# Strassen's seven products for the two branch projections of a hybrid diffusion trunk layer

## The reference

```python
def trunk_layer(x, mod, s_af, s_ab, s_bf, s_bb, col_major, p):
    shift, scale, gate = jnp.split(mod, 3, axis=-1)
    h = rmsnorm(x, p['norm_w']) * (1 + scale) + shift
    proj = h @ p['w_in']
    ...
    o_a, sfa, sba = gdn_branch(qkv, z_a, gate_cols, p, s_af, s_ab)
    o_b, sfb, sbb = lru_branch(x_b, z_b, p, s_bf, s_bb, col_major)
    pa = o_a @ p['w_proj_a']          # (1152 x 1024) @ (1024 x 1024)
    pb = o_b @ p['w_proj_b']          # the same shape
    g_a, g_b = jnp.split(jax.nn.sigmoid(h @ p['w_gate'] + p['b_gate']), 2, axis=-1)
    mixed = (g_a * pa + g_b * pb) @ p['w_out']
    return x + gate * mixed, sfa, sba, sfb, sbb
```

## Time and profile before

| | |
|---|---|
| device time, median of 3 runs | 1491.56 us (1488.91 to 1491.62) |
| span of the profiled execution, first to last instruction | 1486.6 us |
| what lies around the span, median less span | 5.0 us |
| PE busy | 1470.7 us (99%) |
| DVE, ACT, POOL busy | 1016.3, 798.8, 350.0 us |
| branch A and B blocks in the trace | 1177.8 to 1377.6 us, 199.8 us |

### The profile page before, as it was taken

One profiled execution on the slowest core, in us unless ns is written; L12 is line 12 of the kernel. 1 busy time (PEld: TensorE's weight loads), 2 busy tenths in 40 slices (PEclk: granted clock), 3 DMA queues, 4 the chain that ended last, 5 costly groups with the idle time before them and its releaser, 6 DMA issues.

```text
span 1486.6 us, 28072 instructions
## 1 busy us (share of the span) xinstructions
PE 1470.7 (99%) x11376; PEld 1414.7 (95%) x11376; DVE 1016.3 (68%) x1815; ACT 798.8 (54%) x1645; POOL 350.0 (24%) x296
## 2 busy tenths in 40 slices
PE   9999999999999999999999999999999999999997
PEld 8899999999999999999899999999999999999886
DVE  5789897988889898888847744744836711544254
ACT  6574857566584857566476564574576500322111
POOL 3122322232232322132211221221221211342110
PEclk9999999999999999999999999999999999999999
DMA  9322121122213112222311221211212531543132
GB/s 322 112 69 90 33 74 54 45 80 63 79 33 110 30 52 81 88 79 89 114 51 46 82 62 49 82 55 56 82 52 90 170 123 43 169 145 105 43 127 99
DMA packets 122435, 127.46 MB, mean 86 GB/s; under 512 B 6745, under 2 KB 105922, under 8 KB 122306
## 3 DMA queue, kind: packets, MB, share of 16 engines
q1 hardware_dynamic: 122018, 125.34, 26.6%
q10 hardware_dynamic: 288, 0.33, 0.1%
HBM read 105.56 MB, written 20.09 MB: 85 GB/s over the span
## 4 chain that ended last, share of the span: by engine, by line
PE 95%; DVE 2%; SPq 1%; DMA 1%; issue 1%; ACT 0%; POOLq 0%; POOL 0%; DVEq 0%
PE mb L136 16%; PE mb L135 16%; PE mb L134 16%; PE db L134 10%; PE db L136 9%; PE db L135 9%; PE db L1374 2%; PE db L1346 2%; PE db L1390 2%; PE db L1363 2%; PE db L1384 2%; PE db L1008 2%; PE db L1315 1%; PE db L1233 1%; PE db L1194 1%; PE db L1298 1%
## 5 line engine op out<-in xcount | busy, mean ns | idle before, releaser
L134 PE MATMUL mb<-h_hi,w_hi 128*128 128x384 f32 x1080 | 363.0, 336 | 0.0
L135 PE MATMUL mb<-h_lo,w_hi 128*128 128x384 f32 x1080 | 362.9, 336 | 0.0
L136 PE MATMUL mb<-h_hi,w_lo 128*128 128x384 f32 x1080 | 362.9, 336 | 0.0
L134 PE MATMUL db<-h_hi,w_hi 128*128 128x384 f32 x816 | 287.9, 353 | 0.2 <-DVE w_lo L1472 0.2
L136 PE MATMUL db<-h_hi,w_lo 128*128 128x384 f32 x816 | 274.6, 336 | 0.0
L135 PE MATMUL db<-h_lo,w_hi 128*128 128x384 f32 x816 | 274.5, 336 | 0.0
L2074 POOL TENSOR_TENSOR w_lo<-w,w_hi 128x1024 fp32r<-128x1024 f32 x47 | 127.3, 2709 | 459.4 <-ACT w_hi L2109 459.4
L134 PEld LDWEIGHTS mb<-h_hi,w_hi 128*128 128x128 f32 x1080 | 203.0, 188 | 0.1
L136 PEld LDWEIGHTS mb<-h_hi,w_lo 128*128 128x128 f32 x1080 | 203.0, 188 | 0.0
L135 PEld LDWEIGHTS mb<-h_lo,w_hi 128*128 128x128 f32 x1080 | 203.0, 188 | 0.0
L134 PEld LDWEIGHTS db<-h_hi,w_hi 128*128 128x128 f32 x816 | 153.7, 188 | 4.1 <-DVE w_lo L1472 0.7
(11 more groups left out here) (339 smaller groups left out, 2909.4 us busy)
## 6 DMA issues: line engine op xcount, KB each, us to landing
w<-in_w_in SPq DMA_DIRECT2D x48, 512.0 KB, 4.0
d_dt<-decay_rows SPq DMA_DIRECT2D x16, 576.0 KB, 6.7
d_qg<-decay_rows SPq DMA_DIRECT2D x16, 512.0 KB, 4.1
w<-in_w_gate SPq DMA_DIRECT2D x16, 512.0 KB, 4.1
branch_a<-d_kq SPq DMA_DIRECT2D x8, 576.0 KB, 3.3
branch_b<-l_z SPq DMA_DIRECT2D x8, 576.0 KB, 2.8
merge_gates_b<-l_gates SPq DMA_DIRECT2D x8, 576.0 KB, 5.5
m_in<-merge_gates_b SPq DMA_DIRECT2D x8, 576.0 KB
```

The costliest lines, as they stand in the source:

```text
L134: pe.matmul(out, hi, rhi, start=(k == 0), stop=False)
L135: pe.matmul(out, hi, rlo, start=False, stop=False)
L136: return pe.matmul(out, lo, rhi, start=False, stop=(last and stop))
```

## The change

Each branch projection is cut into halves of input channels, output channels and tokens (`KH` = 4 tiles, `TH` = 576 tokens). Instead of eight products of quarters, seven products of sums and differences of quarters are made (Strassen's, in the order 5, 1, 7, 2, 4, 3, 6). A *phase* is one product, with four *items*, one for each tile p of output channels in the half; 2 branches by 7 products by 4 = 56 items w. An item is two banks s of 288 tokens by 4 input tiles by 3 passes = 24 matmuls of 288 columns.

What is new for each item:

- SP loads one or two weight quarters (128x512 each, 256 KB); four raw buffers, `wst` and a new `m_w`.
- POOL forms the weight's sum or difference (`w_sums`, L2164 of the new file, 128x512) for products 5, 1, 7, 2 and 6, and the low part (L2156, 128x512) for all; in its program the sum of an item stands ahead of the low part of the item before.
- ACT makes the high part, 128x512.
- DVE forms the sum of activation quarters (`part_sum`, 128x576) for products 1, 7, 4, 3 and 6 into the `xt` region, and the low part (`part_low`, 128x576), two phases ahead.
- Results leave PSUM in 128x288 pieces: ACT copies them into the accumulator `m_acc` for products 5, 1 and 2, DVE adds them (`add_up`) for products 7, 2, 4, 3 and 6. Products 7 and 6 are accumulated in PSUM on top of the product before them.
- When a tile of the accumulator is complete DVE folds it with the gate from SBUF: `fold_a` (128x1152), `fold_b` (two of 128x1152).

The output projection begins at the last item's end; its weights come through the same four raw buffers, and `mixed` tiles are put in other slots of the activation buffers (`home`).

```diff
+        ORDER = (5, 1, 7, 2, 4, 3, 6)
+        COPIES = {5: ((0, 1, 1.0), (0, 0, -1.0)), 1: ((1, 1, 1.0),), 2: ((1, 0, 1.0),)}
+        ADDS = {7: ((0, 0, ADD),), 2: ((1, 1, SUB),), 4: ((1, 0, ADD), (0, 0, ADD)), 3: ((0, 1, ADD),), 6: ((1, 1, ADD),)}
+        BEHIND = (7, 6)
+        feed = list(range(LAST)) + [NW] + list(range(LAST, NW)) + [NW + k for k in range(1, KT)]
...
+        def wait_ring(eng, w):
+            eng.wait_ge(S["mm"], mm_at(w - 4, 1) if w >= 4 else (NB - 1 + w // 2) * NG)
...
+            for n, item in enumerate(feed):
+                if is_sum(item):
+                    pool.wait_ge(S[raw_sem(n)], raw_count(n))
+                    wait_ring(pool, item)
+                    pool.tensor_tensor(ring(W.wsum, item), raw_of(n)[:, 0:KH, :], raw_of(n)[:, KH:KT, :],
+                                       W_PARTS[combos[item][1]][1]).then_inc(S["w_sum"], 1)
+                if n:
+                    feed_low(n - 1)
...
+            for w in range(NW):
+                if w:
+                    copy_out(w - 1)
...
+                if w + 3 < NW:
+                    feed_high(w + 3)
...
+                if w + 2 * KH < NPH * KH:
+                    part_high(w + 2 * KH)
+                if w >= LAST:
+                    mixed_high(w - LAST)
...
+            def seventh(w):
+                pe.wait_ge(S["w_lo"], was["w_lo"] + NB + at_feed[w] + 1)
+                for s in range(2):
...
+                    for j in range(KH):
+                        if p == 0 and s == 0:
+                            pe.wait_ge(S["r_lo"], was["r_lo"] + n * KH + j + 1)
+                        pe.matmul(out, hi, rhi, start=(j == 0 and m not in BEHIND), stop=False, skip_group_check=True)
+                        pe.matmul(out, hi, rlo, start=False, stop=False, skip_group_check=True)
+                        mm = pe.matmul(out, lo, rhi, start=False, stop=(j == KH - 1), skip_group_check=True)
...
+            for w in range(NW + 1):
+                if w:
+                    add_up(w - 1)
...
+                q = w + 2 * KH
+                if q <= NPH * KH:
+                    part_low(q - 1)
+                if q < NPH * KH:
+                    part_sum(q)
+                if 5 * KH < w <= 7 * KH:
+                    fold_a(w - 5 * KH - 1)
+                elif LAST - KH < w <= LAST:
+                    fold_b(w - LAST + KH - 1)
+                elif w > LAST:
+                    mixed_low(w - LAST - 1)
+            for k in range(KH, KT):
+                fold_b(k)
+                mixed_low(k)
```

More of the change, by code:

```diff
@@ L28 @@
 TAPS, PAD_L = 4, 2
+KH, TH, SW = KT // 2, TOK // 2, TOK // 4
 GAP = TAPS - 1
@@ new lines, in tail_stage @@
+        at_feed = {item: n for n, item in enumerate(feed)}
+        is_sum = lambda item: item < NW and W_PARTS[combos[item][1]][1] is not None
+        n_sums = lambda n: sum(is_sum(item) for item in feed[:n])
+        raw_of = lambda n: wst[:, n % 4] if n % 4 < 2 else wst2[:, n % 4 - 2]
+        raw_sem = lambda n: f"w_in{(NB + n) % 2 if n % 4 < 2 else n % 4}"
+        raw_parts = lambda item: len(W_PARTS[combos[item][1]][0]) if item < NW else 1
+        raw_count = lambda n: (16 * len(range((NB + n) % 2, NB, 2)) if n % 4 < 2 else H * NG) + 16 * sum(
+            raw_parts(feed[i]) for i in range(n % 4, n + 1, 4))
@@ new lines, in part_high @@
+            def part_high(q):
+                n, j = divmod(q, KH)
+                br, m = phases[n]
+                parts, op = R_PARTS[m]
+                if op is not None:
+                    act.wait_ge(S["r_sum"], was["r_sum"] + n_rsums(n) + j + 1)
+                    ins = act.activation(part_hi(n, j), part_sums(n, j), ACT.Copy)
+                else:
+                    act.wait_ge(S[f"r_in{quad_n[parts[0]]}"], quad_count(parts[0], br))
+                    wait_part(act, n, j)
+                    ins = act.activation(part_hi(n, j), quads[parts[0]][:, j, :], ACT.Copy)
+                ins.then_inc(S["r_hi"], 1)
@@ new lines, in copy_out @@
+            def copy_out(w):
+                br, m, p = combos[w]
+                for s in range(2 if m in COPIES else 0):
+                    act.wait_ge(S["mm"], mm_at(w, s))
+                    if br:
+                        act.wait_ge(S["folded"], was["folded"] + p + 1 + (m != 5) * KH)
+                    elif m == 5 and s == 0:
+                        if p == 0:
+                            act.wait_ge(S["out"], was["out"] + 2 * H)
+                        elif p == 2:
+                            act.wait_ge(S["store"], was["store"] + 16 * H)
+                        elif p == 3:
+                            act.wait_ge(S["gb_out0"], 16 * KT // 2)
+                            act.wait_ge(S["gb_out1"], 16 * KT // 2)
+                    for i, l, sign in COPIES[m]:
+                        act.activation(acc_of(p, i, l, s), sum_bank(p, s)[:, 0:SW], ACT.Copy, scale=sign
+                                       ).then_inc(S["copied"], 1)
@@ L2442, in tail_vector, with part_sum @@
-            mixed_low(KT - 1)
+            def part_sum(q):
+                n, j = divmod(q, KH)
+                br, m = phases[n]
+                parts, op = R_PARTS[m]
+                if op is None:
+                    return
+                if j == 0:
+                    for part in parts:
+                        dve.wait_ge(S[f"r_in{quad_n[part]}"], quad_count(part, br))
+                wait_part(dve, n, j)
+                dve.tensor_tensor(part_sums(n, j), quads[parts[0]][:, j, :], quads[parts[1]][:, j, :], op
+                                  ).then_inc(S["r_sum"], 1)
```

451 lines of the change are left out of this document (269 added, 182 removed).

## The result

The changed kernel takes 1505.76 us (median of 4 runs, 1504.71 to 1507.5), the kernel before 1490.24 in the same session (4 runs, 1488.76 to 1491.62): ratio 1.0105, 95% interval 1.0091 to 1.012. It is 1% slower. The forecast was 1486, its range 1475 to 1503.

A forecast was written before the change was run, and what follows sets the result against it. PE was taken to bound the kernel (busy 1470.7 of 1486.6 us). Its 21.6 us saving, less waits of 3.7, 9.1 and 3.3 us for POOL, left 5.5 us gained: median 1491.6 becomes 1486 us, range 1475 to 1503.

The forecast's parts named there:

- PE's term: Branch stage: 1344 matmuls of 288 columns at 0.1325 us take 178.1 us, 21.6 us less than 199.7.
- The price of a turn: DVE and POOL exclude each other at SBUF; a DVE turn costs POOL 0.55 us for 576 columns, 1.15 for 1152.
- Eighteen cycles: ...: Middle, items 24 to 41: POOL's eighteen cycles take 69.5 us against PE's 60.4, 9.1 us of waiting.
- PE waits for POOL's low part: Branch stage: PE's waits between items are for POOL's low part of the weights (L2156), 16 us in all.
- so PE should not see it by itself: Product 4: DVE up to 6 us behind, but banks are reused 9.5 us after the addition falls due.
- The three clusters: PE's waits fall in the first 14 items (3.7 us), items 24 to 41 (9.1) and 52 to 54 (3.3).
- The sum: Whole kernel: 21.6 us saved less 3.7, 9.1 and 3.3 of waits gives 5.5 us gained, 1486 us.
- DVE itself becomes the bound: Rival: product 4's items put DVE behind, 2 to 4 us more, 1489 or so; 0.06 together with loads and clock.
- A late load: Rival: branch A's last phases, two queued quarters outlast the lead, 3 to 7 us more; 0.06 together with two others.
- The clock falls: Rival: new waits between items bring 1.2 GHz, 3 us more per item on it; 0.06 together with two others.
- Averaged away: Rival: DVE and POOL turns slide into shorter items, under 10 us lost, 1474 to 1480 us; chance 0.17.
- Full-duration turns: Rival: items 24 to 40 and 49 to 54, turns cost full durations, 1495 to 1504 us; chance 0.22.

The follow-up runs named there:

- Experiment 11: Changed kernel with activation high and low parts two items later, item 1's load issued early, and folds on 8 of 1152 columns: 1472.3 us, ratio 0.9879 to before.
- Experiment 1: Changed kernel with ACT's high and DVE's low parts of a later product's activation sums made two items later: 1494.6 us, ratio 1.003 to before.
- experiment 2: Changed kernel with item 1's weight load issued ahead of those of items 2 and 3: 1501.7 us, ratio 1.0079 to the kernel before.
- experiment 7: Changed kernel with idle matmuls keeping PE busy in its four longest waits: 1506.5 us, ratio 1.0109 to the kernel before.
- 12: Changed kernel with activation parts one item later, item 1's load early and branch A's folds one product later: 1489.1 us, ratio 0.9992 (0.9983 to 1.0001) to before.
- experiment 4: Changed kernel with POOL's weight sums on 8 columns only and the parts made from the first quarter: 1487.5 us, ratio 0.9984 to the kernel before.
- experiment 3: Changed kernel with the three fold instructions on 8 of 1152 columns: 1492.5 us, ratio 1.0018 to the kernel before.
- experiment 6: Changed kernel with activation parts one item later and item 1's load issued early: 1491.1 us, ratio 1.0009 to the kernel before.

## Why the prediction was wrong, by its own steps

**PE's term: right.** 0.1327 us for 288 columns against 0.1325, 178.3 us against 178.1. Experiment 11 confirms it as a gain: 183.3 us less 3.9 of waits and 1.1 of slow matmuls is 178.3.

**The price of a turn: right.** The groups of the kernel after, beside the earlier trace rows:

```profile
L2156 POOL TENSOR_TENSOR w_lo<-w_sums,w_hi 128x512 fp32r<-128x512 f32 x40 | 69.6, 1744 | 11.2 <-ACT w_hi L2201 11.2
L2588 DVE TENSOR_TENSOR h_lo<-xt,h_hi 128x576 fp32r<-128x576 f32 x40 | 46.9, 1172 | 11.2 <-ACT h_hi L2224 11.0
L2603 DVE TENSOR_TENSOR m_acc<-m_acc,mb 128x288 f32<-128x288 f32 x96 | 38.1, 443 | 8.9 <-issue 4.4 <-PE mb L2445 4.4
L2607 DVE SCALAR_TENSOR_TENSOR mixed<-mixed,m_acc 128x1152 f32<-128x1152 f32 x8 | 16.2, 2026 | 0.0
```

POOL's 512 takes 1.28 us alone (forecast 1.25), 1.80 with a 576 turn and 2.39 with an 1152 turn: 0.52 and 1.11 us a turn, forecast 0.55 and 1.15. `add_up` takes 0.443 us beside whatever runs.

**The step that failed** is "Eighteen cycles: ..." with what stands ahead of it, "PE waits for POOL's low part", read as if POOL's cycle alone set when that part is ready; and the rival's sentence "so PE should not see it by itself". I priced what DVE costs POOL and never DVE's own sum, in which POOL's part of each turn comes back. DVE is held for 3.88 us in an item of product 4 (I had said 3.3 and up to 1.25 more, so its size was on the page) and for 4.72 in one with a `fold_b`; over the stage it is busy for 189.8 us, more than PE's 178.3. Its work alone would fit: 89 instructions of 576 at 0.75 us, 92 of 288 at 0.44 and 18 of 1152 at 1.35 are 132 us, an estimate from the shortest durations. Most of the rest is standing for POOL. Nor did I read ACT's program for what stands behind a wait on DVE. I cleared DVE's lateness by the reuse of PSUM banks only, while the way that it took was ACT's `part_high` ahead of `feed_high`, the high part of the weight, and from there POOL's low part. Experiment 1 shows it: with that way open PE gets 11.2 us back and product 4's items take DVE 3.18 us.

**The three clusters.** They lie roughly where the forecast put them, with other sizes and partly other causes (forecast in brackets). Start 3.6 us (3.7, near by luck: one wait ahead of item 2, from item 1's load, experiment 2, and not POOL's cycle over 14 items). Items 21 to 32 13.4 (9.1 for 24 to 41). Items 46 to 54 10 (3.3). At the end POOL's sum for item 52 stood behind a low part that waited for ACT, and item 52's own low part behind that of the `w_out` weight and one more sum:

```profile
1363.13 1.27 POOL L2156 TENSOR_TENSOR w_lo<-m_w,w_hi 128x512 fp32r<-128x512 f32 x1 [2.60 <-ACT w_hi L2205]
1367.01 1.28 POOL L2156 TENSOR_TENSOR w_lo<-m_w,w_hi 128x512 fp32r<-128x512 f32 x1 [2.60 <-ACT w_hi L2205]
1368.25 1.81 POOL L2164 TENSOR_TENSOR w_sums<-w 128x512 f32<-128x512 f32 x1
1370.02 3.47 POOL L2153 TENSOR_TENSOR o_w_lo<-w,o_w_hi 128x1024 fp32r<-128x1024 f32 x1
```

PE had finished item 48, whose buffer that sum takes, at 1359.9; the sum starts at 1368.25. The starts of the low parts, 3.88 apart, are the ring of product 4 again, now in branch B.

**The sum.** Forecast: 16.1 us lost against 21.6 gained. Measured: 28.7 of waits and 8.9 of slow matmuls against 21.4, 16.2 longer; the medians differ by 15.5, the spans by 16.6. Three sums of the prediction are off besides, without bearing on this: at its cheapest prices the middle adds up to 1.6 us lost and not 3.3, so the good end is 1473; 10 us lost give 1480 and not 1478; and 8.5 us more over some 85 turns are 0.10 each, not 0.15.

**The rivals.** "DVE itself becomes the bound" came nearest, at 0.06 together with two others: it has the right engine and product 4, but not the way through ACT, and its 2 to 4 us were far too few. "A late load" was right too, for the one at the start, where SP's order and not the bandwidth made it late. "The clock falls": it did, I saw nothing for it, and in the stage it cost nothing of its own (experiment 7). "Averaged away" happens in the first four phases, where experiment 2 loses 2 us in all. "Full-duration turns" gave nearly the right time (1503) for a wrong reason: the turns cost what was forecast.

**What stays open.** No full version beats the kernel before by what can be told: 12's interval ends at 1.0001. Between 12 (302.0 us of stage and output; its profiled execution, span 1491.1, also began the stage 2.8 us late) and 11 (284.0) lie the folds' 24 instructions and one item of delay of the parts. A version that takes them from DVE and keeps the rest should be faster by the same reasoning; it wasn't tried. How 4's gain divides between POOL's time and the turns that DVE no longer waits was not separated, nor 3's between DVE's time and POOL's turns.

## What to carry to other kernels

When work goes from the bound engine to helpers, add up each helper's time per item, its turns at a shared port included, and compare it with the bound engine's new item, phase by phase: the one that is over is the new bound, however many buffers lie between. Then follow every in-order program, the idle engine's above all, for early work that waits for a late engine and stands ahead of urgent work. Where such waits close to a ring, the ring sets the pace though each engine's own work fits: here 3.88 us, with 2.80 of DVE's. And price an order by stage and successor together: a wait removed here may be waited for at the next stage.

## What the runs showed of the hardware

- When DVE's 576 and POOL's 512 want SBUF at once, one stands for the other: POOL's 512 grows by 0.52 us for a 576 turn, DVE's 576 from 0.75 to 1.83. The one that came first was not slowed: POOL's low part, 0.06 us ahead at 1250.50, took its 1.28, and so in every item of product 4.
- A DVE instruction can be short and still stand: `fold_a` on 8 columns took 0.16 us alone and 1.25 beside POOL's 512 (experiment 3, six of eight times).
- Turns go both ways: DVE's `mixed` of 1152 took 3.39 us at 1371.31 beside POOL's 1024 of 3.47, against 1.36 with POOL idle (1402.91).
- In the kernel after, PE's matmuls were 0.24 us apart for 11 to 22 in a row behind waits of 2.2 us and more, which is the level of 1.2 GHz, and at 0.13 behind waits of up to 1.7 us. The wait's length alone doesn't tell: behind 2.6 us ahead of item 31 in experiment 6 and 2.3 ahead of item 52 in experiment 4 they stayed at 0.13. In a stage that another engine sets, the lower level cost nothing (experiment 7).
- A matmul of 288 columns lies on the straight line between 256 and 384: 0.1189, 0.1327, 0.1733 us.
